# GpSimd's unit split moved to ScalarE and VectorE, and three adaLN units moved ahead of the odd layer

## The chip, the cores and the metric

One NeuronCore of a Trainium2 chip runs the whole kernel. The time is device microseconds of one execution. Engine names here: TensorE is PE, VectorE is DVE, ScalarE is ACT, GpSimd is POOL, and SP is the queue that issues the weight loads.

## What is computed

Two token streams, 128 context tokens and 256 latent tokens, pass through two trunk layers of width 1024. The kernel handles them together as 384 tokens, in float32. Every layer draws six modulation vectors per stream from an adaLN projection (`w_ada`, 1024 x 6144), then does a mixer and a squared-ReLU MLP:

```python
for li in range(DEPTH):                                        # DEPTH = 2
    sh1, sc1, g1, sh2, sc2, g2 = ada_mods(c, p['w_ada'][li], p['b_ada'][li])
    h = rms_norm(x, p['norm_w'][li, 0]) * (1 + sc1) + sh1
    if li % 2 == 0:
        y = even_layer(h)      # gated linear recurrence + windowed attention
    else:
        y = odd_layer(h)       # q, k, v = split_cols(h @ w_in_odd); differential attention, 8 heads
    x = x + g1 * y
    h = rms_norm(x, p['norm_w'][li, 1]) * (1 + sc2) + sh2
    x = x + g2 * sq_relu_mlp(h, p['w_mlp1'][li], p['w_mlp2'][li])
```

## The kernel before

**Units.** Every large weight is cut into units of 1024 x 256 (1 MB): 97 of them, numbered in order of use. Units 17 to 48 are the first MLP (four groups of eight), 49 to 60 the odd layer's input projection (q, k and v of four pairs of heads; "unit 0 of the odd layer" is 49), 61 to 64 its output projection, 65 to 96 the second MLP. Beside these there are 48 adaLN units of the same size, a0 to a47; a24 to a47 belong to the odd layer, and a36 to a47 (shift, scale and gate of its MLP) are used only behind its attention.

**A unit's way.** SP loads it into one of four places of `raw` (`load`, L468). A product is made at more than bfloat16 precision by splitting both factors into a high and a low part: the high part of the weights is a copy `wH <- raw` (ACT, `split_high`, L1035, and L1040 in the rows), the low part `wL = raw - wH` (DVE, `split_low`, L1486, L1493 in the rows), which raises the semaphore `w_split`. Then TensorE runs three passes over eight k tiles (`gemm_tiles`, L568; the rows' L594 for the "tok" form of 72 matmuls a unit, L589 for the other). `wH` and `wL` hold two units, so the split of unit u waits until the matmuls of unit u-2 are done. One unit of all is split by GpSimd: unit 50, `split` at L1956, called behind the last GpSimd work of the first MLP.

**An adaLN unit's way.** It needs no split: `ada_mm` (L604) runs 16 small matmuls from `raw` into a PSUM bank (OB for a0 to a35, TB for a36 to a47), ACT copies the row (`ada_copy`, L1046), `ada_turn` (L616) transposes it in two matmuls into TB, and DVE reduces it and adds the bias (`ada`, L1496: two small operations, L1505 and L1508). The copy on ACT frees the place in `raw`.

**The order of loads.** `STREAM` (L66 to L75) lists units and adaLN units in the order of loading; `POS` is the index in it. An item goes to place `pos % 4`. SP issues the loads one behind the other, each with a wait on the item four positions earlier: on `w_split` for a unit, on the copy of ACT for an adaLN unit. Around the change the list is 49, 50, a36, 51, a37, 52, a38, 53, and so on.

**Between the MLP and the odd layer.** DVE adds the last residual, ACT squares the last two tiles of x, TensorE sums the squares over the partitions with a matrix of ones (`last_norm_sums`, L637), ACT makes `rstd`. Then DVE's `modulate` (L1544) goes over eight tiles: `scaled_tile` (L1523, L1529 in the rows) multiplies, ACT's `shift` (L1090) adds and rounds to the high part of the operand, and `low_tile` (L1533, L1539 in the rows) makes its low part, which lets TensorE run that k tile of unit 49. The last residual waits on the last unit of the MLP, and so do ACT's and GpSimd's splits of unit 50.

**The odd layer's loop.** In each of its 12 units TensorE runs four k tiles, then turns and attention steps that are due, `ada_mm(36 + u)`, then the other four k tiles; the previous adaLN unit is turned behind the second k tile (L966 to L983). Attention of a pair of heads runs beside units 3 to 11. ACT and DVE have the same steps in the same order, each in its own loop (L1403, L1889).

Of the kernel before, what the change touches and what calls it, by code (L numbers as in the profile page):

```python
# [31 lines left out]
KT = D // P  # L32
# [36 lines left out]
    STREAM += [("a", _a) for _a in adas_of(_u)] + [("u", _u + 2)]  # L69
STREAM += [("a", _a) for _a in TAIL_ADAS]  # L70
STREAM += [("u", _u) for _u in range(15, U_ODD + 2)]
for _i in range(12):
    STREAM += [("a", 36 + _i), ("u", U_ODD + 2 + _i)]
STREAM += [("u", _u) for _u in range(U_ODD + 14, N_UNITS)]
POS = {item: n for n, item in enumerate(STREAM)}  # L75

POOL_UNITS = [U_ODD + 1]


def high_count(u):  # L80

    return u + 1 - sum(n <= u for n in POOL_UNITS)

# [73 lines left out]
def psum_uses():  # L159

    sc, tb, ob = [], ["vecs0", "vecs1"], []
    tb += [f"x{k}" for k in range(0, KT, 2)]
    sc += [f"x{k}" for k in range(1, KT, 2)] + ["norm0"]
    for a in ADA_FIRST:
        tb.append(f"ada{a}")
        ob.append(f"ada{a}")

    def even_jobs(jobs):
        for name in jobs:
            kind, i = job(name)  # L170
            if kind == "hg":
                sc.append(name)
            elif kind == "ada":
                ob.append(name)
            elif kind == "adt":
                tb.append(f"ada{i}")
            elif kind == "tq":
                sc.append(name)
            elif kind == "tk":
                tb.append("tk")  # L180
            elif kind == "swaA":
                if i >= 3:
                    ob.append(f"swaO{i - 3}")
                if i < N_SWA + 2:
                    tb.append(f"swaP{i - 2}.0")
            elif kind == "swaB":
                if i >= 2:
                    tb.append(f"swaP{i - 2}.1")
                if i < N_SWA:
                    sc.append(f"swa{i}")  # L190
            elif kind == "tile":
                sc.append(name)
                tb.append(f"turned{i}")
            elif kind == "state":
                ob.append(name)
            elif kind == "hgO":
                ob.append(name)
            elif kind == "hgN":
                tb.append(name)

    for jobs in EVEN_JOBS:
        even_jobs(jobs)
    even_jobs(EVEN_TAIL)
    sc.append("norm1")
    sc.append("norm2")

    def diff(s):
        if s >= 18 and norm_due(s):
            tb.append(f"dN{(s - 3) // 3}")
        if 2 <= s < N_DIFF + 2:  # L210
            tb.append(f"dP{s - 2}")
        if s < N_DIFF:
            sc.append(f"d{s}")
        if s >= 2 and (s - 2) % 3 == 2:
            ob.append(f"dO{(s - 2) // 3}")

    for u in range(13):
        for half in range(2):
            if half == 0 and u:
                tb.append(f"ada{35 + u}")  # L220
            if u < 12:
                tb.extend([f"dN{(s - 3) // 3}" for s in odd_slots(u, half) if norm_due(s)])
            if half == 0:
                tb.extend(odd_turns(u, 0))
                if u == 12:
                    tb.extend(odd_turns(u, 1))
            for s in odd_slots(u, half):
                diff(s)
            if u < 12:
                tb.extend(odd_turns(u, 1) if half else [f"adaM{36 + u}"])  # L230
    sc.append("norm3")
    tb.extend([f"y{k}" for k in range(KT)])
    return [{name: n for n, name in enumerate(uses)} for uses in (sc, tb, ob)]
# [31 lines left out]
def step_backbone_kernel(nc, t):  # L265
    ctx = ExitStack()
    with ctx:
# [157 lines left out]
            sem(n) for n in ("const_in", "x_in", "vec_in", "even_in", "odd_in", "out_dma", "kd_out"))  # L425
        raw_in = [sem(f"raw_in{i}") for i in range(RAW)]

        w_high, pool_high, w_split, gemm_done = (sem(n) for n in ("w_high", "pool_high", "w_split", "gemm_done"))

        g_free = [sem(f"g_free{i}") for i in range(2)]  # L430
        sc_full, sc_free = sem("sc_full"), sem("sc_free")
# [35 lines left out]
        def _(sp):  # L467
            def load(src, pos, wait=None):  # L468


                if wait is not None:
                    sp.wait_ge(*wait)
                elif pos >= RAW:
                    kind, n = STREAM[pos - RAW]
                    if kind == "u":
                        sp.wait_ge(w_split, n + 1)
                    elif n < 36:
                        sp.wait_ge(ob_free, OB_USE[f"ada{n}"] + 1)
                    else:
                        sp.wait_ge(tb_free, TB_USE[f"adaM{n}"] + 1)  # L480
                sp.dma_start(raw[:, pos % RAW, :, :], src).then_inc(raw_in[pos % RAW], 16)
# [73 lines left out]
        def _(pe):  # L555
# [48 lines left out]
            def ada_mm(a):  # L604

                pos = POS["a", a]
                buf, out, done, name = ("ob", OB, ob_full, "ada") if a < 36 else ("tb", TB, tb_full, "adaM")
                pe.wait_ge(raw_in[pos % RAW], 16 * (pos // RAW + 1))
                take(buf, f"{name}{a}")
                for k in range(KT):  # L610
                    j = k % 4
                    mm = pe.matmul(out[32 * j:32 * j + 32, 0:UC], cst[:, k, :], raw[:, pos % RAW, k, :],  # L612
                                   start=k < 4, stop=k >= 4, skip_group_check=True, tile_position=(0, 32 * j))
                mm.then_inc(done, 1)

            def ada_turn(a):  # L616

                if a < 36:
                    pe.wait_ge(ob_free, OB_USE[f"ada{a}"] + 1)
                take("tb", f"ada{a}")  # L620
                for i in range(2):
                    mm = turn(TB[:, P * i:P * i + P], adarow[:, P * i:P * i + P])
                mm.then_inc(tb_full, 1)
# [276 lines left out]
            with pe.Fori(0, 2) as g:  # L900
                mlp_group(U_MLP0 + 8, g, 2 * KT, 4, MLP0_ORDER)
            mlp_group(U_MLP0 + 24, 0, 2 * KT, 12, MLP0_ORDER)
            last_norm_sums(2)


            def diff_norm(s):
# [59 lines left out]
            for u in range(12):  # L966
                for half in range(2):
                    middle = {}
                    if u and half == 0:
                        middle[1] = lambda: ada_turn(35 + u)  # L970
                    if odd_slots(u, half):
                        middle[2] = lambda: diff_norm(odd_slots(u, half)[0])
                    gemm_half(U_ODD + u, half, "tok", (opH, opL), op_ready(3 * KT) if u == 0 else None,
# [2 lines left out]
                        turns(u, 0)  # L976
                    for s in odd_slots(u, half):
                        diff(s)
                    if half == 0:
                        ada_mm(36 + u)  # L980
                    else:
                        turns(u, 1)
            ada_turn(47)  # L983
            turns(12, 0)
            turns(12, 1)

# [29 lines left out]
        def _(act):  # L1016
# [27 lines left out]
                    split_high(u, POS["u", u])  # L1044

            def ada_copy(a):  # L1046
                if a < 36:
                    full("ob", f"ada{a}")
                    act.activation(adarow[:, :], OB[:, 0:UC], ACT.Copy).then_inc(ob_free, 1)
                else:  # L1050
# [270 lines left out]
            def mlp_group(base, g, pos, n_hid, last, turned_out=None, finish=None):  # L1321


                for i in range(8):
# [17 lines left out]
                        split_high(u + 2, pos + i + 2, g)  # L1342
                    if turned_out is not None and i > 4:
                        turned_out(2 * (i - 5) + 1)
                    if finish is not None and i >= 4:
                        finish(u, 2 * (i - 4))

# [4 lines left out]
            with act.Fori(0, 2) as g:  # L1352
                mlp_group(U_MLP0 + 8, g, b0 + 8, 4, False)
            mlp_group(U_MLP0 + 24, 0, b0 + 24, 12, False,
                      finish=lambda u, tile0: squares(2, u, tile0))
            norm_rstd(2)
            shift(2)


            act.wait_ge(lamr_set, 1)  # L1360
# [42 lines left out]
            for u in range(12):  # L1403
# [2 lines left out]
                turned(u, 0)  # L1406
                for s in odd_slots(u, 0):
                    diff(s)
                ada_copy(36 + u)
                for s in odd_slots(u, 1):  # L1410
                    diff_norm(s)
                g = unit_out(U_ODD + u, "tok")
# [60 lines left out]
        def _(dve):  # L1473
# [12 lines left out]
            def split_low(u, g=0, pos=None):  # L1486

                pos = POS["u", u] if pos is None else pos
                dve.wait_ge(w_high, high_count(u) + 8 * g)
                if u - 1 in POOL_UNITS:  # L1490

                    dve.wait_ge(w_split, u)
                dve.tensor_tensor(wL[:, u % 2, :, :], raw[:, pos % RAW, :, :], wH[:, u % 2, :, :].bitcast(F32),  # L1493
                                  ALU.subtract).then_inc(w_split, 1)

# [45 lines left out]
                                                   opH[:, q, a:b].bitcast(F32), ALU.add, ALU.subtract)  # L1541
                ins.then_inc(op_set, 1)

            def modulate(n, n_op):  # L1544

                dve.wait_ge(rstd_set, n + 1)
                for k in range(KT + 1):
                    if k < KT:
                        scaled_tile(n, n_op, k)
                    if k:  # L1550
                        low_tile(n, n_op, k - 1)

# [300 lines left out]
                mlp_group(0, U_MLP0 + 8, g, b0 + 8, 4, False)  # L1853
            mlp_group(0, U_MLP0 + 24, 0, b0 + 24, 12, False, 2)
            scales(2, 32)
            modulate(2, 3 * KT)


            dve.wait_ge(odd_in, 16 * 3)
# [29 lines left out]
            for u in range(12):  # L1889
# [6 lines left out]
                    dve.wait_ge(g_free[(U_ODD + u) % 2], (U_ODD + u) // 2 + 1)  # L1896
                for s in odd_slots(u, 1):
                    diff(s)
                ada(36 + u)
                split_low(U_ODD + u + 2)  # L1900
                if part < 2:
                    qk_scale(draw[:, part, :], 3 + 2 * j + part + 1, 12)
# [27 lines left out]
        def _(pool):  # L1930
# [21 lines left out]

            settle(pool.tensor_scalar(wrow[:, 2, :], wrow[:, 2, :], HD ** -0.5, None, ALU.mult))
            settle(tables(ropeE, 0))

            def split(u):  # L1956


                pos = POS["u", u]
                pool.wait_ge(raw_in[pos % RAW], 16 * (pos // RAW + 1))  # L1960
                if u >= 2:
                    pool.wait_ge(gemm_done, u - 1)
                pool.tensor_scalar(wH[:, u % 2, :, :], raw[:, pos % RAW, :, :], 1.0, None, ALU.mult).then_inc(pool_high, 1)
                pool.wait_ge(pool_high, POOL_UNITS.index(u) + 1)

                pool.wait_ge(w_split, u)
                pool.tensor_tensor(wL[:, u % 2, :, :], raw[:, pos % RAW, :, :], wH[:, u % 2, :, :].bitcast(F32),
                                   ALU.subtract).then_inc(w_split, 1)

            def keys(u):  # L1970

# [81 lines left out]
            with pool.Fori(0, 4) as g:  # L2053
                relu_squares(U_MLP0, g, 0)

            split(U_ODD + 1)

            pool.wait_ge(rope_tab, 1)
            for j in range(4):
                for part in range(2):  # L2060
# [80 lines left out]
```

## Time and profile before

| | before |
|---|---|
| median of 3 runs | 1167.46 us (1167.18 to 1168.17) |
| profiled execution | 1167.8 us |
| its span | 1165.7 us |
| PE busy | 1054.6 us (90%), 7330 matmuls |
| DVE busy | 571.7 us (49%) |
| ACT busy | 486.8 us (42%) |
| POOL busy | 144.5 us (12%) |
| mean granted TensorE clock | 0.966 of full |
| loads | 160.38 MB moved, mean 138 GB/s |

Times in rows are microseconds from the start of the span. "Idle before <-releaser" says how long an engine had nothing to do ahead of a row, and whose work let it go on. "Landing" is the time from the issue of a load until its data is there. PEclk is the granted clock: 1.00 is 2.4 GHz, 0.50 is 1.2 GHz.

### The profile page before, as it was taken

The numbers are of one execution on the slowest core, as the hardware profiler recorded it, in microseconds if no ns is written. First come the engines' busy times: TensorE is split into PE (matmuls) and PEld (weight loads), VectorE is DVE, ScalarE is ACT, GpSimd is POOL, SyncE is SP. The second block draws the span as 40 slices with busy tenths as digits, with TensorE's granted clock in tenths as the row PEclk, the third lists the DMA queues.
The fourth block names the chain that finished last, engine by engine and source line by source line (L and its number), as shares of the span: only waits on it lengthen the run. The fifth ranks groups of instructions, "written<-read, shape, count | busy, mean of one in ns | idle before, by whom it ended". The sixth has DMA issues, their size and how long they took to land.

```text
span 1165.7 us, 17989 instructions
## 1 busy us (share of the span) xinstructions
PE 1054.6 (90%) x7330; PEld 963.1 (83%) x7330; DVE 571.7 (49%) x906; ACT 486.8 (42%) x858; POOL 144.5 (12%) x170
## 2 busy tenths in 40 slices
PE   5798677788889999999996998999789999999998
PEld 2686455667789999999996987777579999999997
DVE  2543535655346544445456535555645544445452
ACT  4345344434435425243343535555535414334241
POOL 0051101000010102010013123113000101011010
PEclk9999898899999999999999999999889999999999
DMA  8865333366462443434332444443213343434321
GB/s 284 279 200 207 109 109 109 112 238 208 149 222 81 137 145 109 144 109 136 116 129 90 144 155 144 145 150 120 83 39 107 123 138 109 138 111 140 110 72 55
DMA packets 157099, 160.38 MB, mean 138 GB/s; under 512 B 3627, under 2 KB 155717, under 8 KB 157029
## 3 DMA queue, kind: packets, MB, share of 16 engines
q1 hardware_dynamic: 155028, 156.50, 40.9%
q0 software_dynamic: 528, 1.70, 0.4%
q10 hardware_dynamic: 1472, 1.18, 0.3%
q8 instruction: 52, 0.85, 0.3%
q14 instruction: 19, 0.15, 0.0%
HBM read 156.09 MB, written 3.28 MB: 137 GB/s over the span
## 4 chain that ended last, share of the span: by engine, by line
PE 76%; ACT 12%; DVE 7%; issue 4%; DMA 0%; SPq 0%; ACTq 0%; DVEq 0%
PE G L589 54%; PE G L594 10%; ACT wH L1040 3%; PE OB L612 3%; PE TB L563 3%; DVE wL L1493 1%; PE OB L946 1%; PE OB L792 1%; PE TB L612 1%; DVE small L1731 1%; PE SC L632 1%; DVE nbuf L1529 1%; ACT hq L1187 1%; PE SC L675 1%; PE SC L681 1%
## 5 line engine op out<-in xcount | busy, mean ns | idle before, releaser
L589 PE MATMUL G<-opH,wH 128*128 128x386 f32 (+1 forms) x768 | 273.2, 356 | 5.5 <-DVE wL L1493 3.1
L589 PE MATMUL G<-opH,wL 128*128 128x386 f32 (+1 forms) x768 | 264.8, 345 | 0.0
L589 PE MATMUL G<-opL,wH 128*128 128x386 f32 (+1 forms) x768 | 264.7, 345 | 0.0
L1040 ACT ACTIVATE wH<-raw 128x2048 fp32r<-128x2048 f32 x96 | 183.3, 1910 | 186.8 <-PE G L589 182.7
L1493 DVE TENSOR_TENSOR wL<-raw,wH 128x2048 fp32r<-128x2048 f32 x96 | 221.1, 2303 | 80.9 <-ACT wH L1040 80.9
L589 PE MATMUL G<-hidH,wH 128*128 128x384 f32 x512 | 172.5, 337 | 0.0
L589 PE MATMUL G<-hidH,wL 128*128 128x384 f32 x512 | 172.1, 336 | 0.0
L589 PE MATMUL G<-hidL,wH 128*128 128x384 f32 x512 | 172.1, 336 | 0.0
L589 PEld LDWEIGHTS G<-opH,wH 128*128 128x128 f32 x768 | 148.6, 194 | 16.9 <-issue 8.5
L589 PEld LDWEIGHTS G<-opL,wH 128*128 128x128 f32 x768 | 148.4, 193 | 0.9
L589 PEld LDWEIGHTS G<-opH,wL 128*128 128x128 f32 x768 | 148.4, 193 | 0.0
L594 PE MATMUL G<-wH,opH 128*128 128x256 f32 x408 | 124.7, 306 | 15.1 <-DVE opL L1539 13.9
L594 PE MATMUL G<-wH,opL 128*128 128x256 f32 x408 | 117.2, 287 | 0.0
L594 PE MATMUL G<-wL,opH 128*128 128x256 f32 x408 | 116.9, 287 | 0.0
L1584 DVE SCALAR_TENSOR_TENSOR xT<-G,mods,xT 128x128 f32<-128x128 f32 (+1 forms) x160 | 55.7, 411 | 124.2 <-PE G L589 124.2
L2050 POOL TENSOR_TENSOR relu<-relu 128x768 f32<-128x768 f32 x32 | 47.0, 1469 | 535.7 <-ACT relu L1336 535.7
L1336 ACT ACTIVATE relu<-relu,small 128x128 f32<-128x128 f32 (+1 forms) x128 | 48.0, 447 | 150.9 <-DVE relu L1833 150.9
L594 PEld LDWEIGHTS G<-wH,opH 128*128 128x128 f32 x408 | 79.7, 195 | 27.6 <-issue 20.4
L589 PEld LDWEIGHTS G<-hidL,wH 128*128 128x128 f32 x512 | 96.3, 188 | 0.0
L589 PEld LDWEIGHTS G<-hidH,wH 128*128 128x128 f32 x512 | 96.3, 188 | 0.0
L589 PEld LDWEIGHTS G<-hidH,wL 128*128 128x128 f32 x512 | 96.2, 188 | 0.0
L594 PEld LDWEIGHTS G<-wH,opL 128*128 128x128 f32 x408 | 79.7, 195 | 0.7
(244 smaller groups left out, 1161.5 us busy)
## 6 DMA issues: line engine op xcount, KB each, us to landing
raw<-in_w_mlp SPq DMA_DIRECT2D x64, 1024.0 KB, 5.2
raw<-in_w_ada SPq DMA_DIRECT2D x48, 1024.0 KB, 6.3
raw<-in_w_in_even SPq DMA_DIRECT2D x13, 1024.0 KB, 6.5
raw<-in_w_in_odd SPq DMA_DIRECT2D x12, 1024.0 KB, 5.0
raw<-in_w_out_even SPq DMA_DIRECT2D x4, 1024.0 KB, 5.3
raw<-in_w_out_odd SPq DMA_DIRECT2D x4, 1024.0 KB, 5.2
xin<-in_x_sample SPq DMA_DIRECT2D x1, 1024.0 KB, 6.4
out_y_sample<-yout SPq DMA_DIRECT2D x1, 768.0 KB, 4.0
```

The costliest lines, as they stand in the source:

```text
L563: return pe.transpose(out, src, ident[0:n, 0:n])
L589: mm = pe.matmul(G[:, s, 512 * m:512 * m + cols], w[:, s, k, P * m:P * m + P], a[:, k, 0:cols], start=first and q == 0, stop=last and q == 2)
L594: mm = pe.matmul(G[:, s, UC * tt:UC * tt + UC], a[:, k, P * tt:P * tt + P], w[:, s, k, :], start=first and q == 0 and tt != 1, stop=last a ...
L612: mm = pe.matmul(out[32 * j:32 * j + 32, 0:UC], cst[:, k, :], raw[:, pos % RAW, k, :], start=k < 4, stop=k >= 4, skip_group_check=True, ti ...
L632: mm = pe.matmul(SC[:, 0:NTOK], ones[:, :], rstd[:, :] if k == 5 else nbuf[:, k % 2, :], start=k == 5, stop=k == KT - 1)
L675: mm = pe.matmul(SC[:, P * m:P * m + P], hq[:, n, :], joined(n, 2 ** lev), start=True, stop=True, skip_group_check=True)
L681: mm = pe.matmul(SC[c:c + 32, 32 * m:32 * m + 32], k, q, start=True, stop=True, skip_group_check=True, tile_position=(0, c))
L1040: act.activation(wH[:, u % 2, :, :], raw[:, pos % RAW, :, :], ACT.Copy).then_inc(w_high, 1)
L1336: ins = act.activation(part, part, ACT.Relu, bias=shifts[:, u % 2, m, c:c + 1])
L1493: dve.tensor_tensor(wL[:, u % 2, :, :], raw[:, pos % RAW, :, :], wH[:, u % 2, :, :].bitcast(F32), ALU.subtract).then_inc(w_split, 1)
L1584: ins = dve.scalar_tensor_tensor(xT[:, k, a:b], G[:, u % 2, 512 * m + a:512 * m + b], mods[:, layer, KT * gate + k, c:c + 1], xT[:, k, a:b ...
L2050: pool.tensor_tensor(relu2[:, u % 2, :], relu[:, u % 2, :], relu[:, u % 2, :], ALU.mult).then_inc(relu2_set, 1)
```

## The change

Unit 50 is split by ACT (high part, in the last unit of the first MLP, ahead of the last two squares) and by DVE (low part, behind the whole modulation). GpSimd splits nothing. Three adaLN units, a36 to a38, are computed between the first MLP and the odd layer, with bank OB instead of TB: TensorE puts a36 between the sums of squares and a37, a38 behind them; ACT copies them around `norm_rstd` and the first shifts; DVE takes a36 ahead of the modulation and a37 and a38 within it. The odd layer's loop does a39 to a47 in its units 0 to 8, none in 9 to 11. `STREAM` follows: 49, 50, a36, a37, a38, 51, a39, 52, a40, 53 and so on.

```diff
@@ STREAM
 STREAM += [("u", _u) for _u in range(15, U_ODD + 2)]
+STREAM += [("a", 36), ("a", 37), ("a", 38)]
 for _i in range(12):
-    STREAM += [("a", 36 + _i), ("u", U_ODD + 2 + _i)]
+    STREAM += [("u", U_ODD + 2 + _i)] + ([("a", 39 + _i)] if _i < 9 else [])
...
@@ SP, load
                     if kind == "u":
                         sp.wait_ge(w_split, n + 1)
-                    elif n < 36:
+                    elif n < 39:
                         sp.wait_ge(ob_free, OB_USE[f"ada{n}"] + 1)
...
@@ TensorE, behind the first MLP
-            last_norm_sums(2)
+            norm_sum(2, 5)
+            ada_mm(36)
+            norm_sum(2, 6)
+            norm_sum(2, 7)
+            ada_turn(36)
+            ada_mm(37)
+            ada_turn(37)
+            ada_mm(38)
...
@@ TensorE, the odd layer's loop
-                    if u and half == 0:
-                        middle[1] = lambda: ada_turn(35 + u)
+                    if u <= 9 and half == 0:
+                        middle[1] = lambda: ada_turn(38 + u)
...
-                    if half == 0:
-                        ada_mm(36 + u)
-                    else:
+                    if half:
                         turns(u, 1)
-            ada_turn(47)
+                    elif u < 9:
+                        ada_mm(39 + u)
...
@@ ACT, mlp_group
+                    if finish is not None and i == 7:
+                        split(U_ODD + 1)
                     if finish is not None and i >= 4:
                         finish(u, 2 * (i - 4))
...
+            ada_copy(36)
             norm_rstd(2)
-            shift(2)
+            ada_copy(37)
+            shift(2, range(2))
+            ada_copy(38)
+            shift(2, range(2, KT))
...
@@ DVE
-            def modulate(n, n_op):
+            def modulate(n, n_op, adas):
                 dve.wait_ge(rstd_set, n + 1)
                 for k in range(KT + 1):
                     if k < KT:
                         scaled_tile(n, n_op, k)
+                    if k in adas:
+                        ada(adas[k])
                     if k:
                         low_tile(n, n_op, k - 1)
...
             scales(2, 32)
-            modulate(2, 3 * KT)
+            ada(36)
+            modulate(2, 3 * KT, {1: 37, 4: 38})
+            split_low(U_ODD + 1)
...
@@ GpSimd
-            split(U_ODD + 1)
```

## Rows read from the trace of the kernel before

**Rows 1.** page, part 4: the chain that ended last, its share of the span by engine
```profile
PE 76%; ACT 12%; DVE 7%; issue 4%; DMA 0%; SPq 0%; ACTq 0%; DVEq 0%
```

**Rows 2.** chain of waits, 628 to 700: start us, us, engine, output and line, count
```profile
634.37 0.81 DVE nbuf L1529 x3
...
635.29 4.72 DVE nbuf L1529
...
640.82 7.12 PE G L594 x36
647.94 1.00 PE TB L612 x16
...
659.09 1.07 PE TB L612 x16
...
670.56 1.07 PE TB L612 x16
```

**Rows 3.** timeline, 618 to 665, ACT, then GpSimd: start, us, engine, operation, count [idle before <-releaser]
```profile
621.27 1.92 ACT L1040 ACTIVATE wH<-raw 128x2048 fp32r<-128x2048 f32 x1 [5.58 <-PE G L589]
623.09 0.92 ACT L1057 ACTIVATE nbuf<-xT 128x384 f32<-128x384 f32 x2
630.96 0.94 ACT L1057 ACTIVATE nbuf<-xT 128x384 f32<-128x384 f32 x2 [6.95 <-DVE xT L1584]
...
653.45 0.81 ACT L1418 ACTIVATE dsq<-G 128x768 f32<-128x768 f32 x1 [1.92 <-PE G L594]
...
629.66 5.36 POOL L1963 TENSOR_SCALAR wH<-raw 128x2048 fp32r<-128x2048 f32 x1 [29.32 <-PE G L589]
635.11 4.63 POOL L1967 TENSOR_TENSOR wL<-raw,wH 128x2048 fp32r<-128x2048 f32 x1
```

**Rows 4.** timeline of VectorE, 640 to 690
```profile
639.94 0.74 DVE L1539 SCALAR_TENSOR_TENSOR opL<-nbuf,mods,opH 128x128 fp32r<-128x128 f32 x2
640.71 0.75 DVE L1529 SCALAR_TENSOR_TENSOR nbuf<-xT,scale,rstd 128x128 f32<-128x128 f32 x2
...
649.55 0.75 DVE L1539 SCALAR_TENSOR_TENSOR opL<-nbuf,mods,opH 128x128 fp32r<-128x128 f32 x2 [0.22 <-ACT opH L1096]
...
655.93 0.17 DVE L1505 TENSOR_REDUCE small<-TB 128x4 f32<-128x16 f32 x1
...
656.79 2.29 DVE L1493 TENSOR_TENSOR wL<-raw,wH 128x2048 fp32r<-128x2048 f32 x1 [0.49 <-ACT wH L1040]
```

**Rows 5.** timeline of the SP queue, 590 to 720: the issues of weight loads
```profile
625.53 0.37 SPq L481 DMA_DIRECT2D raw<-in_w_ada  x1
639.76 0.37 SPq L481 DMA_DIRECT2D raw<-in_w_in_odd  x1
...
659.11 0.37 SPq L481 DMA_DIRECT2D raw<-in_w_in_odd  x1
```

**Rows 6.** loads issued at 72.4 and 72.8, then 84.7 and 85.1: us to landing, min/median/max
```profile
L481 SPq DMA_DIRECT2D raw<-in_w_ada x2: 367/474/582, 72.4 to 72.8; - x2
...
DMA to landing us min/median/max: 5.4/6.6/7.7
...
DMA to landing us min/median/max: 5.1/6.2/7.3
```

**Rows 7.** windows: us, PE, PEld, DVE, ACT, POOL busy, PEclk, DMA share, GB/s
```profile
56.00:57.00 1.00, 0.84 (x4) 0.84 (x5) 0.80 (x3) 0.02 (x1) 0.00 (x0) 0.58 1.01 323
59.00:60.00 1.00, 1.00 (x8) 1.00 (x8) 0.00 (x0) 0.00 (x0) 0.66 (x2) 0.72 1.09 388
636.00:637.00 1.00, 0.00 (x0) 0.00 (x0) 1.00 (x1) 0.00 (x0) 1.00 (x1) 0.71 0.00 0
646.00:647.00 1.00, 1.00 (x8) 1.00 (x7) 0.96 (x4) 0.62 (x2) 0.00 (x0) 0.67 0.00 0
```

**Rows 8.** chain of waits, 762 to 862, units 9 to 11 of the odd layer
```profile
777.50 1.00 PE TB L612 x16
...
798.20 0.28 ACT adarow L1052
```

More of the change, by code:

```diff
@@ L71 @@
 STREAM += [("u", _u) for _u in range(15, U_ODD + 2)]
+STREAM += [("a", 36), ("a", 37), ("a", 38)]
 for _i in range(12):
-    STREAM += [("a", 36 + _i), ("u", U_ODD + 2 + _i)]
+    STREAM += [("u", U_ODD + 2 + _i)] + ([("a", 39 + _i)] if _i < 9 else [])
 STREAM += [("u", _u) for _u in range(U_ODD + 14, N_UNITS)]
 POS = {item: n for n, item in enumerate(STREAM)}
-POOL_UNITS = [U_ODD + 1]
 def high_count(u):
-    return u + 1 - sum(n <= u for n in POOL_UNITS)
+    return u + 1
 N_HG = 2 * (LEVELS + 1)
@@ L205, in psum_uses @@
     sc.append("norm2")
+    for a in (36, 37, 38):
+        ob.append(f"ada{a}")
+        tb.append(f"ada{a}")
     def diff(s):
@@ L218, in psum_uses @@
         for half in range(2):
-            if half == 0 and u:
-                tb.append(f"ada{35 + u}")
+            if half == 0 and 1 <= u <= 9:
+                tb.append(f"ada{38 + u}")
             if u < 12:
@@ L229, in psum_uses @@
             if u < 12:
-                tb.extend(odd_turns(u, 1) if half else [f"adaM{36 + u}"])
+                tb.extend(odd_turns(u, 1) if half else [f"adaM{39 + u}"] if u < 9 else [])
     sc.append("norm3")
@@ L426, in step_backbone_kernel @@
         raw_in = [sem(f"raw_in{i}") for i in range(RAW)]
-        w_high, pool_high, w_split, gemm_done = (sem(n) for n in ("w_high", "pool_high", "w_split", "gemm_done"))
+        w_high, w_split, gemm_done = (sem(n) for n in ("w_high", "w_split", "gemm_done"))
         g_free = [sem(f"g_free{i}") for i in range(2)]
@@ L606, in ada_mm @@
                 pos = POS["a", a]
-                buf, out, done, name = ("ob", OB, ob_full, "ada") if a < 36 else ("tb", TB, tb_full, "adaM")
+                buf, out, done, name = ("ob", OB, ob_full, "ada") if a < 39 else ("tb", TB, tb_full, "adaM")
                 pe.wait_ge(raw_in[pos % RAW], 16 * (pos // RAW + 1))
@@ L616, in ada_turn @@
             def ada_turn(a):
-                if a < 36:
+                if a < 39:
                     pe.wait_ge(ob_free, OB_USE[f"ada{a}"] + 1)
@@ L1046, in ada_copy @@
             def ada_copy(a):
-                if a < 36:
+                if a < 39:
                     full("ob", f"ada{a}")
@@ L1408, in _ @@
                     diff(s)
-                ada_copy(36 + u)
+                if u < 9:
+                    ada_copy(39 + u)
                 for s in odd_slots(u, 1):
@@ L1489, in split_low @@
                 dve.wait_ge(w_high, high_count(u) + 8 * g)
-                if u - 1 in POOL_UNITS:
-                    dve.wait_ge(w_split, u)
                 dve.tensor_tensor(wL[:, u % 2, :, :], raw[:, pos % RAW, :, :], wH[:, u % 2, :, :].bitcast(F32),
@@ L1898, in _ @@
                     diff(s)
-                ada(36 + u)
+                if u < 9:
+                    ada(39 + u)
                 split_low(U_ODD + u + 2)
@@ L1954, in _ @@
             settle(tables(ropeE, 0))
[L1956 to L1968, printed above, removed]
             def keys(u):
```

## The prediction

> **What bounds the kernel now.** I read the page first: the chain that ended last is TensorE for 76% of the span, and ACT, VectorE (DVE) and issue for nearly all the rest [rows 1]. TensorE alone is therefore the measure: a change pays where it shortens a stretch in which TensorE is idle or does extra work, and costs where TensorE waits longer. The chain in order of time then shows the stretch that the change touches [rows 2]. The last MLP matmul ends near 629.5, DVE starts the modulation at 634.37, one DVE operation of that group takes 4.72 us, and the first matmul of the odd layer starts at 640.82. It runs four k tiles until 647.94, then the adaLN unit 36 (16 matmuls), then the rest. The timelines of ACT and GpSimd say what lies beside it [rows 3]: GpSimd splits unit 50 from 629.66 to 639.74. The SP queue's timeline says which load goes out when [rows 5].
>
> **Part 1, GpSimd's split goes: a gain before the odd layer.** The slow DVE operation (L1529, 128x256) takes 4.72 us while GpSimd's two-input subtract runs (635.11 to 639.74); a pair of the same line (128x128 and 128x256) takes 0.75 us once GpSimd is quiet [rows 2 to 4]. It ends when GpSimd ends. Two pairs would need 2 x 0.75, overlapped by a little, so 1.4 us instead of the 5.6 from 634.37 to 640.0: 4.1 us less.
> The Trainium skill, page "SBUF — State Buffer", section "SBUF: two separate sides", says the same: the port pair of DVE and GpSimd is an exclusive lock, and a DVE operation with two SBUF inputs blocks for a whole GpSimd instruction. The trace agrees (4.72 us). A reading that stops there forecasts 4.1 us of gain and nothing else.
>
> **Part 2, ACT takes the high split of unit 50.** It stands before the last two squares. It waits for the end of unit 48, as GpSimd did. In the group before, the squares follow a split 1.82 us after its start (621.27, 623.09) [rows 3]. A split from 629.6 puts the squares at 631.42 instead of 630.96: 0.46 us later, all of it on the path square, sum, rstd, modulation. DVE then starts at 634.37 + 0.46 = 634.83.
>
> **Part 3, three adaLN units in the gap.** On TensorE unit 36 fits between the sums (one takes 1.00 [rows 2]; TensorE idles there), and 37 and 38 run while DVE modulates. The copies on ACT fall into its waits. DVE's share is two small operations, 655.93 to about 656.3 [rows 4], 0.35 us each unit. Unit 36 lies in the wait for rstd: free. Unit 37 stands before the first low tile and 38 after the fifth scaled tile: 0.35 each on the DVE path. The first low tile starts at 634.83 + 1.4 + 0.35 = 636.6 (before 639.94 [rows 4]), so TensorE could start the odd layer 3.4 us earlier.
>
> **Part 4, DVE takes the low split, behind the modulation.** Before, the modulation ran from the first low tile at 639.94 to the end of the last, 649.55 + 0.75 = 650.30 [rows 4], 10.36 us. Now: 636.6 + 10.36 + 0.35 (unit 38) = 647.3, and the split, 2.29 us [rows 4], ends at T = 649.6. Before, GpSimd had it done at 639.74. If the adaLN unit 38 reaches DVE late, because TensorE turns it only after its second k tile, T is up to 1 us later.
>
> **Part 5, what is queued behind that split: the term that decides.** SP issues the weight loads strictly in the order of STREAM, and each waits until the item four places earlier is used up. Before, the order was 49, 50, a36, 51, a37, 52: the load of a36 needed nothing of unit 50. The load behind unit 50's split was unit 52, issued at 639.76, 0.02 after GpSimd's end [rows 3, 5], with time to spare. Now the order is 49, 50, a36, a37, a38, 51, a39, 52, a40. Unit 51 stands four behind unit 50, so its load waits for T. a39 needs only a36, long done, but it stands behind 51 in SP's queue. And TensorE runs a39 in the middle of the first unit of the odd layer (unit 49), where a36 ran. TensorE finishes its first four k tiles by about 644 at the latest and then stands. a38's load, last issued before, goes out at 625.53 as a37's did [rows 5] and is in time.
> The landing: of two loads issued 0.4 us apart the second landed 7.7 us after its issue, the first 5.4 (issued at 72.4 and 72.8); in another such pair 5.1 and 7.3 [rows 6]. I take 7.5, with 7.3 and 7.7 as ends. a39: 649.6 + 0.03 + 0.4 + 7.5 = 657.5. The same place in the kernel before is 647.94 [rows 2]: **+9.6 us**. The gain of parts 1 to 3 is gone with it: it only lengthens the stand.
> Two more loads (52, a40) are issued at once behind a39. The Trainium skill, page "DMA: Bandwidth & Descriptors", section "Queues, rings and completion order", says that each DMA engine takes descriptors in ring order, so they should not delay a39; the pair of 72.4 had a third load behind it as well and still landed in order. Without ring order a39 would land up to about 5.5 us later (a rival below).
>
> **Part 6, TensorE's clock.** The granted clock is half (1.2 of 2.4 GHz) after the gap of the kernel before: it fell within 636 to 637, while TensorE waited for the modulation, and rose within 646 to 647, though TensorE was at work from 640.82: 5.9 us of work at half rate [rows 2, 7]. That cost lay in the first four k tiles. Now the stand of 13 us or more falls behind them, so the clock falls again and a39 and the second half of unit 49 (36 matmuls, from 648.94 to ACT's start on it at 653.45 [rows 2, 3]) pay it: 5.9 / 2 = 2.9 us. The nearest short case is 56 to 60 us, about 3.2 us at half: 1.6 [rows 7]. I take **2.9**, since the idle before it is like the long one; ends 1.6 and 3.0.
>
> **Part 7, what goes out of the last three units.** Units 9 to 11 of the odd layer lose their adaLN matmuls, and 10 and 11 their turns. On the chain there: 1.00 at 777.50, the same once more in unit 11, 0.28 of ACT's copy at 798.20 [rows 8] and one turn of about 0.2. The third set of matmuls (unit 10) is hidden behind DVE and ACT, and so is the last turn. **-2.5 us**; ends -1.0 (TensorE waits for ACT and DVE instead) and -3.0. Units 1 to 8 keep one adaLN unit each. The tightest is now that of unit 2: its load follows that of unit 53, which went out at 659.11 (behind unit 51's split), and TensorE wants it at 670.56 [rows 2, 5], 11.4 us later where 0.4 + 7.5 are needed: no wait, nothing.
>
> **Sum.** +9.6 + 2.9 - 2.5 = +10.0 us on the profiled execution (1167.8, span 1165.7): 1177.8. The median before is 1167.46, 0.3 lower; so 1177.5.
>
> **Rivals.**
> (a) The load is in time, and the kernel is faster. It decides at about 643.5: a39 must have landed when TensorE's fourth k tile is done, so its load must be out by 636, before DVE has even begun the low tiles. Then TensorE starts 3.4 us earlier, but in unit 50 it waits for ACT, which stands at unit 51's load (landing 649.6 + 5, split until 656.5) before it copies the turned keys; before, that wait ended at 659.09 [rows 2] and now near 658.6. So -0.5, and with part 7 -3.0: 1164.5. For it speaks only that I could misread the order; the measured 0.02 from split to load speaks against.
> (b) The loads share the engines evenly. Each further 1 MB moved the landing by about 2.7 us (72.4 + 5.4 to 72.8 + 7.7) [rows 6]; a39 would land with the fourth, 5.5 us later: 1183.0. The landings in order speak against.
> (c) The removed work of part 7 gives 1 us alone, or the clock stays low for the short spell: 1179.0 and 1176.2, both within my case's own range.
> (d) The stand is shorter by some overlap that I don't see and the two gains nearly cancel it, within 0.2% of before: a39 would have to start by 651, when its load is hardly out.
>
> **How the numbers follow.** My case 0.80, (a) 0.06, (b) 0.08, (d) 0.03, and 0.03 for a larger loss still. My case's own range: low 9.3 + 1.6 - 3.0 = +7.9, high 10.8 + 3.0 - 1.0 = +12.8, so 1175.4 to 1180.3. For 8 in 10 with room for (b) I give 1174.0 to 1183.0. 0.2% is 2.3 us, about what a measurement of this kernel can tell from no change. Faster 0.06, same 0.03, slower 0.91.
>
> **What would show it.** Right: SP's load of unit 51 within 0.1 us behind DVE's split near 649.6, and not at 617; TensorE idle from about 643 until near 657.5 in front of the adaLN matmuls; half clock behind it; DVE's L1529 at 0.75 a pair; first matmul of the layer near 637.3. Wrong: the adaLN matmuls in unit 49 before 650 (part 5), a39 landing after 660 (b), full clock behind the stand (part 6), units 9 to 11 no shorter (part 7).

## The result, and the profile after

The changed kernel took 1175.74 us (median of 8 runs, 1171.59 to 1179.99), the kernel before 1167.14 (median of 8, 1163.04 to 1170.68). The ratio is 1.0086, 95% interval 1.0065 to 1.0108: slower by 10.0 us (0.0086 x 1167; the ratio compares runs of the same chip, and the two medians differ by 8.6). The profiled execution took 1179.53 with a span of 1177.6. Line numbers have moved: L1504 is the low split (before L1493), L1540 the scaled tile (L1529), L1550 the low tile (L1539), L613 the adaLN matmuls (L612), L595 the "tok" matmuls (L594), L1047 the high split (L1040).

The page of the kernel after, span and busy time. Nothing of it says where 12 us of span went: TensorE does 1.8 us more and GpSimd 10 us less than before.

```profile
span 1177.6 us, 17991 instructions
...
PE 1056.4 (90%) x7330; PEld 962.7 (82%) x7330; DVE 567.2 (48%) x907; ACT 487.8 (41%) x859; POOL 134.3 (11%) x168
```

To compare two executions, one must first take out what lies ahead of the change. Both kernels have the same program up to the last residual of the first MLP, but for the order in which SP takes its last loads. That residual starts at 629.53 before and at 632.06 after (VectorE's timelines: before's row is in the next fence, after's is the first row of the one behind it), 2.53 us apart. The change hardly made this: the variants below whose program is the changed kernel's up to there start it between 625.93 and 628.93. I call this start R, and count from it.

```profile
629.53 1.39 DVE L1584 SCALAR_TENSOR_TENSOR xT<-G,mods,xT 128x128 f32<-128x128 f32 x4 [2.89 <-PE G L589]
630.84 2.48 DVE L1516 SCALAR_TENSOR_TENSOR scale<-mods,vecs 128x16 f32<-128x16 f32 x1
```

VectorE's timeline of the kernel after, start and duration in front. It answers to [rows 2, 4].

```profile
632.06 1.39 DVE L1597 SCALAR_TENSOR_TENSOR xT<-G,mods,xT 128x128 f32<-128x128 f32 x4 [2.89 <-PE G L590]
633.37 0.16 DVE L1527 SCALAR_TENSOR_TENSOR scale<-mods,vecs 128x16 f32<-128x16 f32 x1
...
637.26 1.41 DVE L1540 SCALAR_TENSOR_TENSOR nbuf<-xT,scale,rstd 128x128 f32<-128x128 f32 x4 [0.52 <-ACT rstd L1076]
...
638.88 0.75 DVE L1550 SCALAR_TENSOR_TENSOR opL<-nbuf,mods,opH 128x128 fp32r<-128x128 f32 x2
...
648.77 0.75 DVE L1550 SCALAR_TENSOR_TENSOR opL<-nbuf,mods,opH 128x128 fp32r<-128x128 f32 x2 [0.21 <-ACT opH L1103]
649.44 2.28 DVE L1504 TENSOR_TENSOR wL<-raw,wH 128x2048 fp32r<-128x2048 f32 x1
```

The four scaled operations take 1.41 us instead of 5.65, as GpSimd is quiet. GpSimd's copy had slowed VectorE too: the small operation for the scales (L1516, L1527 after) takes 0.16 us instead of 2.48, and 2.48 again in e3 below, where GpSimd splits. That cost nothing before, since it ended at 633.32 and the scaled operations wait for `rstd` until 634.37. But the split of unit 50 comes last and ends at 651.72, which is R + 19.7; before, GpSimd's ended at R + 10.2 [rows 3].

The SP queue's timeline, which answers to [rows 5]: the load of unit 51, a39, unit 52, a40.

```profile
651.75 0.37 SPq L482 DMA_DIRECT2D raw<-in_w_in_odd  x1
652.16 0.58 SPq L482 DMA_DIRECT2D raw<-in_w_ada  x1
652.79 1.54 SPq L482 DMA_DIRECT2D raw<-in_w_in_odd  x1
654.37 2.63 SPq L482 DMA_DIRECT2D raw<-in_w_ada  x1
```

Unit 51's load goes out 0.03 us behind the end of the split, and a39's 0.4 behind that. The two answers of the trace on landing, first for the loads of 651.75 and 652.16 (min, median, max), then for those of 652.79 and 654.37:

```profile
DMA to landing us min/median/max: 5.2/6.3/7.5
...
DMA to landing us min/median/max: 9.5/10.1/10.7
```

They landed at 657.0, 659.7, 662.3 and 665.1: one behind the other, 2.7 us apart. TensorE's timeline: the first k tile of unit 49, the last matmul of its fourth, and a39.

```profile
639.77 0.35 PE L595 MATMUL G<-wH,opH 128*128 128x256 f32 x1 [0.56 <-DVE opL L1550]
...
645.34 0.28 PE L595 MATMUL G<-wL,opH 128*128 128x256 f32 x1
...
659.69 1.94 PE L613 MATMUL TB<-raw,cst 128*32 128x256 f32 x16 [14.07 <-DMA raw<-in_w_ada]
```

The view of who waited for whom, TensorE from 640 to 670 (us in total, times, longest):

```profile
PE TB L613 <- DMA raw<-in_w_ada: 14.1, 1, 14.1
```

This is the cost of the change in one line: TensorE starts the odd layer at R + 7.7 (before R + 11.3), and then stands 14.07 us, until the data of a39 are there. The windows (columns as in [rows 7]) show the clock: full (1.00) in the first k tiles, falling in the stand, half when TensorE resumes, full again from 665.3 (0.84 as the mean of its window).

```profile
639.00:640.00 1.00, 0.44 (x6) 0.26 (x3) 0.96 (x4) 0.80 (x3) 0.00 (x0) 1.00 0.00 0
648.00:649.00 1.00, 0.00 (x0) 0.00 (x0) 0.79 (x3) 0.74 (x2) 0.00 (x0) 0.63 0.00 0
664.00:665.00 1.00, 1.00 (x7) 1.00 (x6) 0.00 (x0) 0.00 (x0) 0.00 (x0) 0.50 0.38 132
665.00:666.00 1.00, 1.00 (x9) 1.00 (x9) 0.00 (x0) 0.00 (x0) 0.00 (x0) 0.84 0.00 0
```

### The profile page after: what moved, and what is told of

The parts are those of the page before. It is cut to its first block and busy times, and to the rows that moved or that the text cites. A ratio compares the mean times of both kernels' runs of the same rounds, so it can differ in the third digit from the quotient of the medians.

```text
span 1177.6 us, 17991 instructions
## 1 busy us (share of the span) xinstructions
PE 1056.4 (90%) x7330; PEld 962.7 (82%) x7330; DVE 567.2 (48%) x907; ACT 487.8 (41%) x859; POOL 134.3 (11%) x168
## 5 line engine op out<-in xcount | busy, mean ns | idle before, releaser
L1047 ACT ACTIVATE wH<-raw 128x2048 fp32r<-128x2048 f32 x97 | 185.1, 1909 | 193.2 <-PE G L590 189.1
L1504 DVE TENSOR_TENSOR wL<-raw,wH 128x2048 fp32r<-128x2048 f32 x97 | 223.3, 2302 | 84.0 <-ACT wH L1047 84.0
L595 PE MATMUL G<-wH,opH 128*128 128x256 f32 x408 | 124.4, 305 | 8.3 <-DVE opL L1550 7.1
L595 PE MATMUL G<-wH,opL 128*128 128x256 f32 x408 | 117.1, 287 | 0.0
L595 PE MATMUL G<-wL,opH 128*128 128x256 f32 x408 | 116.8, 286 | 0.0
L595 PEld LDWEIGHTS G<-wH,opH 128*128 128x128 f32 x408 | 79.4, 195 | 20.6 <-issue 12.4
L595 PEld LDWEIGHTS G<-wH,opL 128*128 128x128 f32 x408 | 79.6, 195 | 0.7
```

The costliest lines, as they stand in the source:

```text
L595: mm = pe.matmul(G[:, s, UC * tt:UC * tt + UC], a[:, k, P * tt:P * tt + P], w[:, s, k, :], start=first and q == 0 and tt != 1, stop=last a ...
L1047: act.activation(wH[:, u % 2, :, :], raw[:, pos % RAW, :, :], ACT.Copy).then_inc(w_high, 1)
```

## The experiments

Every count below is from R of its own execution. "End of unit 49" is the start of ACT's first operation on it, [rows 3] before and the last row here of after; the first two rows are ACT's split of unit 50 and the squares behind it.

```profile
632.12 1.91 ACT L1047 ACTIVATE wH<-raw 128x2048 fp32r<-128x2048 f32 x1 [5.58 <-PE G L590]
633.94 0.92 ACT L1064 ACTIVATE nbuf<-xT 128x384 f32<-128x384 f32 x2
...
667.78 0.81 ACT L1432 ACTIVATE dsq<-G 128x768 f32<-128x768 f32 x1 [5.70 <-PE G L595]
```

| kernel | R | first matmul of unit 49 | end of unit 49 | ratio of times to before, 95% |
|---|---|---|---|---|
| before | 629.53 | 11.3 | 23.9 | 1 |
| after | 632.06 | 7.7 | 35.7 | 1.0086 (1.0065 to 1.0108) |
| e1_split_first | 625.93 | 7.7 | 19.1 | 0.9914 (0.9892 to 0.9935) |
| e2_port_only | 631.30 | 8.9 | 20.7 | 0.9948 (0.9933 to 0.9963) |
| e3_pool_keeps_split | 628.51 | 11.5 | 24.8 | 0.9981 (0.9961 to 1.0001) |
| e4_a39_before_51 | 627.03 | 7.7 | 33.3 | 1.0041 (1.0019 to 1.0063) |
| e5_busy_stand | 628.93 | 7.7 | 34.7 | 1.0092 (1.0059 to 1.0124) |
| e6_gap_busy | 620.61 | 7.7 | 18.8 | 0.9954 (0.9932 to 0.9977) |
| e7_busy_to_landing | 627.54 | 7.7 | 33.2 | 1.0080 (1.0051 to 1.0109) |

**One edit that removes the stand.** DVE is free between its last residual and rstd, so its split fits there.

```diff
             scales(2, 32)
+            split_low(U_ODD + 1)
             ada(36)
             modulate(2, 3 * KT, {1: 37, 4: 38})
-            split_low(U_ODD + 1)
```

> The changed kernel with one edit: DVE makes the low part of unit 50 before the modulation, not behind it. Theory (the load of a39 waits for that split): DVE is free between its last residual and rstd, the split ends about 634 in the time frame of the kernel before (17 us earlier than in the changed kernel), a39 lands near 642, before TensorE's fourth k tile is done near 643, and the stand of 14 us is gone. TensorE then follows DVE's modulation, ends unit 49 about 5.3 us earlier than the kernel before, and with 2.6 us from units 9 to 11 the whole is about 8 us faster than before: 1159, ratio 0.993. Rival (the moved adaLN units and the DVE split themselves cost the time, wherever they stand): it stays within 2 us of the changed kernel, ratio 1.007 to 1.01.

It took 1155.57 us (before on the same chip 1166.14): ratio 0.9914. VectorE's timeline, with the residual and the split, then TensorE's row of a39's matmuls, then ACT's start on unit 49:

```profile
625.93 1.39 DVE L1597 SCALAR_TENSOR_TENSOR xT<-G,mods,xT 128x128 f32<-128x128 f32 x4 [2.89 <-PE G L590]
...
628.00 2.29 DVE L1504 TENSOR_TENSOR wL<-raw,wH 128x2048 fp32r<-128x2048 f32 x1 [0.60 <-ACT wH L1047]
```

```profile
639.44 1.07 PE L613 MATMUL TB<-raw,cst 128*32 128x256 f32 x16
```

```profile
645.00 0.81 ACT L1432 ACTIVATE dsq<-G 128x768 f32<-128x768 f32 x1 [0.38 <-PE G L595]
```

The split now ends at 630.3 (R + 4.4), the loads go out behind it, and a39's matmuls at 639.44 have no wait in front of them. The end of unit 49 is 16.6 us earlier than in the changed kernel, and the first matmul of unit 49 starts no later (R + 7.7 in both). So the moved adaLN units and the DVE split are not what cost the time; the rival has fallen. The gain over the kernel before is 10.0 us (7.6 to 12.6) where 8 was expected; from R to the end of the span the two profiled executions differ by 7.5. Beside e2, which lacks the adaLN units in the gap, e1's median is 4.5 us lower. From R to the first matmul of the output projection their traces differ by 3.1 of it (196.6 and 199.7): 1.6 at the end of unit 49, and 1.5 behind it. Units 9 to 11 are 2.9 us shorter, but e2 has no spell of half clock near 700 and e1 has one. This kernel, with one line moved, beats both.

**The port alone.** The kernel before, with only the split moved.

```diff
-POOL_UNITS = [U_ODD + 1]
+POOL_UNITS = []
...
+                    if finish is not None and i == 7:
+                        split(U_ODD + 1)
                     if finish is not None and i >= 4:
                         finish(u, 2 * (i - 4))
...
             scales(2, 32)
+            split_low(U_ODD + 1)
             modulate(2, 3 * KT)
...
-            split(U_ODD + 1)        # GpSimd
```

> The kernel before with the split of unit 50 alone moved: ACT's part in the last unit of the first MLP, DVE's part before the modulation, GpSimd splits nothing, adaLN units and load order as before. Port theory: L1529 falls from 4.72 to about 0.4 us, the odd layer starts about 3.6 us earlier (4.1 less the 0.46 of ACT's split), and the time is 3.5 to 5 us below before: 1162 to 1164, ratio 0.996. Rival (GpSimd's split hid behind other work): within 1 us of before.

0.9948, 6.1 us faster (4.3 to 7.8), where 3.5 to 5 was expected. VectorE's timeline: the residual, and the four scaled operations, 1.41 us. Then the window that starts at 640:

```profile
631.30 1.39 DVE L1586 SCALAR_TENSOR_TENSOR xT<-G,mods,xT 128x128 f32<-128x128 f32 x4 [2.89 <-PE G L589]
...
637.73 1.41 DVE L1531 SCALAR_TENSOR_TENSOR nbuf<-xT,scale,rstd 128x128 f32<-128x128 f32 x4 [2.06 <-ACT rstd L1069]
```

```profile
640.00:641.00 1.00, 0.76 (x3) 0.80 (x4) 0.96 (x4) 0.10 (x2) 0.00 (x0) 0.50 0.04 12
```

The port theory holds: 5.65 us of the four operations have become 1.41. The modulation starts later here than after an undisturbed sum (R + 6.4, not 5.2), because in this execution the clock had fallen already in the sums of squares: it is half (0.50) from R + 2.7 on, and the last two sums take 2.79 us instead of 1.56. It is still half in the first k tiles of unit 49. So the first matmul of unit 49 comes 2.4 us earlier than before, not 3.6; the end of unit 49 comes 3.2 earlier, and the stretch from R to the end of the span is 4.3 us shorter. Why the whole time gained 6.1 is open.

**The same new order with GpSimd's split.** The function `split` and its semaphore come back with it; they are left out here.

```diff
+POOL_UNITS = [U_ODD + 1]
...
-                    if finish is not None and i == 7:
-                        split(U_ODD + 1)
...
             ada(36)
             modulate(2, 3 * KT, {1: 37, 4: 38})
-            split_low(U_ODD + 1)
...
+            split(U_ODD + 1)        # GpSimd
```

> The changed kernel with the split of unit 50 given back to GpSimd; the three adaLN units and the new load order stay. Theory (the end of that split sets the stand): the split ends at 639.7 in the frame of the kernel before, a39 lands near 647.7, TensorE arrives there at 647 to 648, so the stand is 0 to 1.5 us, not 14. With 2.6 us from units 9 to 11: 1 to 3 us below before, ratio 0.998. Rival (the new load order or the adaLN units in the gap cost the time themselves): 7 us or more above before.

0.9981 (0.9961 to 1.0001), as expected, though the interval just takes in no change. VectorE, GpSimd, the SP queue (unit 51, a39) and TensorE (a39's matmuls):

```profile
628.51 1.39 DVE L1600 SCALAR_TENSOR_TENSOR xT<-G,mods,xT 128x128 f32<-128x128 f32 x4 [2.89 <-PE G L593]
...
633.27 5.66 DVE L1543 SCALAR_TENSOR_TENSOR nbuf<-xT,scale,rstd 128x128 f32<-128x128 f32 x4 [0.52 <-ACT rstd L1079]
```

```profile
634.08 4.56 POOL L1985 TENSOR_TENSOR wL<-raw,wH 128x2048 fp32r<-128x2048 f32 x1
```

```profile
638.67 0.37 SPq L485 DMA_DIRECT2D raw<-in_w_in_odd  x1
639.09 0.58 SPq L485 DMA_DIRECT2D raw<-in_w_ada  x1
```

```profile
647.70 1.07 PE L616 MATMUL TB<-raw,cst 128*32 128x256 f32 x16 [0.61 <-DMA raw<-in_w_ada]
```

The price of the port is back (5.66 us), the split ends at 638.64 (R + 10.1), the loads go out behind it instead of at R + 19.7, and the stand is 0.61 us. Unit 49 ends 0.9 us later than before. The granted clock fell in this longer gap, though the adaLN units ran in it: half from R + 9.5 to R + 16.3. So the order of loads and the adaLN units cost no more than this 0.9 us while the split ends early, and units 9 to 11 are 1.4 us shorter than before, though a half-clock spell (798 to 802) lies in them.

**Which of the waiting loads comes first.**

```diff
 for _i in range(12):
     STREAM += [("u", U_ODD + 2 + _i)] + ([("a", 39 + _i)] if _i < 9 else [])
+    if _i == 0:
+        STREAM[-2:] = STREAM[:-3:-1]
```

> The changed kernel with the first pair of the new load order swapped: a39 ahead of unit 51. Both still wait for the split of unit 50. Theory (ring order: a39 lands first of the four loads issued together): landing 5.1 us after its issue, not 7.5, issue 0.4 us earlier, so the stand is 2.8 us shorter and the time 2.8 us below the changed kernel: ratio to before 1.006. Rival (the loads share the engines evenly): no difference to the changed kernel.

TensorE's row of a39's matmuls, and the trace's answer on its load:

```profile
652.07 1.93 PE L615 MATMUL TB<-raw,cst 128*32 128x256 f32 x16 [11.48 <-DMA raw<-in_w_ada]
```

```profile
L484 SPq DMA_DIRECT2D raw<-in_w_ada x1: 368/368/368, 646.7 to 646.7; - x1
...
DMA to landing us min/median/max: 5.3/5.3/5.3
```

The load lands 5.3 us after its issue instead of 7.5, and the stand is 11.48 us, 2.6 less; unit 49 ends 2.4 us earlier. The time is 1.0041 of before, 4.5 in 1000 (5 us) under the changed kernel, of which the trace shows 2.4 us; the intervals of the two ratios lie just apart, so the size of the gain in the whole time is uncertain. Loads that share the engines evenly would have landed a39 hardly earlier. The Trainium skill, page "DMA: Bandwidth & Descriptors", section "Queues, rings and completion order", has each DMA engine take its descriptors in ring order; this run agrees (a39 lands 5.3 us after its issue as the first of the four loads, 7.5 us as the second).

**The clock in the stand.** 18 extra matmuls before a39 (e5), then 22 (e7, the same edit with 22 for 18):

```diff
                     elif u < 9:
+                        if u == 0:
+                            pe.wait_ge(sc_free, SC_USE["norm2"] + 1)
+                            for _ in range(18):
+                                pe.matmul(SC[:, 0:NTOK], ones[:, :], xT[:, 0, :], start=True, stop=True)
                         ada_mm(39 + u)
```

> The changed kernel with 18 extra matmuls of ones and a tile of x (results unused) in TensorE's stand in front of a39's adaLN matmuls, some 12 us of work at 0.66 us each. Theory (clock term): the granted clock stays full through the stand, the adaLN matmuls take 1.07 instead of 1.94 us and the second half of unit 49 4.3 instead of 6.2 us, so the time is 2.7 us below the changed kernel: ratio to before 1.006. Rival (the clock does not follow TensorE's idleness here): half clock behind the landing as before, no difference to the changed kernel. Rival 2 (the extra work runs past the landing): up to 1 us of the gain is lost.

> As e5_busy_stand with 22 extra matmuls: 18 lasted 10.9 us and left TensorE idle for 2.3 us before the landing, and the clock was at half behind it. 22 last 13.3 us and reach the landing. Theory (clock term of the stand): full clock through the second half of unit 49, whose end comes 33.0 us behind the start of the last residual (35.7 in the changed kernel, 34.7 with 18), so 2.7 us less there. The whole time may hide this, since other half-clock spells move it by as much. Rival: half clock behind the landing again, 34.7 or more.

With 18, TensorE ran dry 2.34 us before the landing, and the clock fell within 0.2 us of its resuming (a mean of 0.78 in that window). TensorE's row of a39's matmuls, and the windows of the resuming and behind it:

```profile
656.44 1.88 PE L613 MATMUL TB<-raw,cst 128*32 128x256 f32 x16 [2.34 <-DMA raw<-in_w_ada]
```

```profile
656.00:657.00 1.00, 0.56 (x8) 0.36 (x12) 0.00 (x0) 0.00 (x0) 0.00 (x0) 0.78 1.08 386
657.00:658.00 1.00, 1.00 (x15) 0.22 (x5) 0.00 (x0) 0.00 (x0) 0.00 (x0) 0.50 1.09 387
```

With 22:

```profile
655.21 1.07 PE L613 MATMUL TB<-raw,cst 128*32 128x256 f32 x16
```

```profile
656.00:657.00 1.00, 1.00 (x14) 0.79 (x7) 0.00 (x0) 0.39 (x1) 0.00 (x0) 1.00 1.09 387
```

The adaLN matmuls take 1.88 us at half and 1.07 at full clock, and unit 49 ends at R + 34.7 and R + 33.2, where 35.7 is the changed kernel's. The extra work of e7 reaches the landing and doesn't run past it: a39's matmuls start at R + 27.7, against R + 27.6 without it. The clock's term is thus 2.5 us, 1.4 of it lost again where the extra work stops too early. In the whole time it can't be seen: 1.0092 and 1.0080 against 1.0086. Of e5 the expectation of 1.006 failed. Its profiled execution was at half clock from 830 to 848, behind the odd layer's loop, where the changed kernel's was from 832 to 840; that such spells hide the gain in the other executions too is not shown.

**The clock in the gap.** The kernel of e2, with 2 extra matmuls between the sums and 5 behind them:

```diff
-            last_norm_sums(2)
+            norm_sum(2, 5)
+            busy(2)
+            norm_sum(2, 6)
+            norm_sum(2, 7)
+            busy(5)
```

> The kernel with only the split moved (e2_port_only) and 7 extra matmuls (results unused) in TensorE's idle time between the first MLP and the odd layer, 2 between the sums and 5 behind them, where the changed kernel has its adaLN units. Theory (the adaLN units in the gap keep the clock up): full clock through unit 49, its end 18.4 us behind the start of the last residual instead of 20.7, the time 2.3 us below that kernel, ratio to before 0.993. Rival (no effect of the clock, unit 49 follows DVE's modulation anyway): 20.7 and 0.995 again.

VectorE's residual (R) and ACT's start on unit 49:

```profile
620.61 1.39 DVE L1595 SCALAR_TENSOR_TENSOR xT<-G,mods,xT 128x128 f32<-128x128 f32 x4 [2.89 <-PE G L589]
```

```profile
639.38 0.81 ACT L1429 ACTIVATE dsq<-G 128x768 f32<-128x768 f32 x1 [0.37 <-PE G L594]
```

Unit 49 ends at R + 18.8, 1.9 us earlier than in the profiled execution of e2, and the clock is full throughout. But the ratio, 0.9954, is that of e2 (0.9948), and the expected 0.993 did not come. The profiled execution of e2 was the slowest of its 11 (1164.99, median 1160.03), so it may be that the clock falls in this gap in some executions only. The effect is shown for two executions, not for the mean.

## Why the prediction was right

It gave 1177.5, range 1174.0 to 1183.0, slower; the median is 1175.74. By its steps, each from R:

- **The port (part 1).** 4.1 us predicted (its own 5.6 and 1.4 give 4.2); the four operations went from 5.65 to 1.41, 4.2. Right.
- **ACT's split (part 2).** 0.46 predicted; the modulation starts at R + 5.20 instead of R + 4.84: 0.36. Right.
- **The adaLN units in the gap (part 3).** First matmul 3.4 us earlier predicted, 3.6 measured. What the step did not say: the clock was full in the first four k tiles, at half before [rows 7]. It was so in every profiled execution that had these units in the gap and no GpSimd split (after, e1, e4, e5, e7). With the split (e3), where the gap is 11.5 us, it fell again, and without the units (e2, a gap of 8.9) too. In none of these traces did it hold without the work in the gap.
- **The end of the split (part 4).** 649.6 predicted in the time frame of before; 651.72 - 2.53 = 649.2. Right.
- **The load behind it (part 5).** 7.5 us to landing predicted, 7.5 measured; a39's matmuls start at R + 27.6 (659.69 - 632.06) instead of a36's at R + 18.3 (before's row is below): +9.3, where +9.6 was predicted, 0.4 of it since the split ended that much earlier than it had said. The experiments set the end of the split to R + 4.4, R + 10.1 and R + 19.7, and the stand was none, 0.61 and 14.07 us. This is the cause.

```profile
647.87 1.07 PE L612 MATMUL TB<-raw,cst 128*32 128x256 f32 x16
```

- **The clock (part 6).** 2.9 predicted. The end of unit 49 moved by 35.7 - 23.9 = 11.8, so 2.5 on top of the 9.3; e7, with the stand kept busy, measures 2.5 too. Right, 0.4 too large. (Its low end, 1.6, came from a spell of "about 3.2 us"; [rows 7] give 3.4, so 1.7.)
- **The last three units (part 7).** -2.5 predicted. ACT's starts on units 8 to 11 of the odd layer, before and then after:

```profile
768.12 0.81 ACT L1421 ACTIVATE dv<-G 128x768 f32<-128x768 f32 x1
...
783.00 0.81 ACT L1418 ACTIVATE dsq<-G 128x768 f32<-128x768 f32 x1 [3.73 <-PE G L594]
...
798.36 0.82 ACT L1418 ACTIVATE dsq<-G 128x768 f32<-128x768 f32 x1
...
815.01 0.81 ACT L1421 ACTIVATE dv<-G 128x768 f32<-128x768 f32 x1
```

```profile
782.68 0.81 ACT L1435 ACTIVATE dv<-G 128x768 f32<-128x768 f32 x1
...
796.36 0.81 ACT L1432 ACTIVATE dsq<-G 128x768 f32<-128x768 f32 x1 [2.81 <-PE G L595]
...
811.45 0.81 ACT L1432 ACTIVATE dsq<-G 128x768 f32<-128x768 f32 x1
...
826.70 0.81 ACT L1435 ACTIVATE dv<-G 128x768 f32<-128x768 f32 x1
```

The three steps are 14.9, 15.4 and 16.7 us before, and 13.7, 15.1 and 15.3 after: -2.9. Over the whole stretch from the end of unit 49 to the first matmul of the output projection it is 180.24 against 177.66: -2.6, as some 0.3 us came in elsewhere.

Sum from R to the end: 1177.6 - 632.06 = 545.5 against 1165.7 - 629.53 = 536.2, +9.4. The ratio gives +10.0 (7.6 to 12.6), the medians +8.6; predicted +10.0. The mechanism and its steps came out; that the total agrees with the ratio to 0.1 us is luck, since the steps measured in the trace add up to 9.3 + 2.5 - 2.6 = 9.2. Rival (a) fell: the load was late, as the order of the queue said. Its side was real only when the split stood elsewhere, as e1 shows, and there the gain was larger than its 3 us: unit 51's load went out at R + 4.4, and the 4.8 us by which unit 49 ends earlier than before are still there at the end of unit 50 (R + 30.3 against 35.1). Rival (b), loads that share evenly, fell with the landings 2.7 us apart and with e4. Nothing came of (c) or (d).

## What to carry to other kernels

When work moves from one engine to another, ask first which queue waits for its end, and what stands behind that wait: here a split that no matmul needed before the end of unit 49 held back a load that TensorE needed in the middle of it. A load order with four buffers ties each load to the release four places earlier; move two items (here a37 and a38) ahead of another, and its wait falls on another item. A gain of a port or an engine upstream of a stand only makes the stand longer; take the stand away, and the same gains count (e1).

## What the runs showed of the hardware that was not expected

- The same program up to R, but for the order of the last loads, reached it at 620.61 us in one execution (e6) and at 632.06 in another (after), with the others between. In the one of 620.61 the granted clock was half for about 27 us ahead of R, in the one of 632.06 for about 44, but others with 48 reached it at 626 (e1) and 630 (before). So the clock accounts for a part, and the rest is open. Counting from R takes this part out, but not the half-clock spells behind R, 23 to 42 us in sum: from R to the end the profiled executions of e1 to e4 differ from before by -7.5, -4.3, +1.1 and +7.1 us, where their ratios give -10.0, -6.1, -2.2 and +4.8. So two single executions of this kernel don't settle 3 us over the whole span; a stretch such as that from R to the end of unit 49, whose clock one can read, does.
- The clock stayed full through the gap of 7.7 us (from R to the first matmul of unit 49) when seven short matmuls (e6) or three adaLN units lay in it, fell in the gap of 8.9 us without either (e2), and fell in the gap of 11.5 us of e3 in spite of the adaLN units.
- Four loads of 1 MB, issued within 2.6 us, land one behind the other, 2.7 us apart. A place further ahead in the queue gave a39 2.2 us from its own issue, and 2.6 us of stand (e4).
- VectorE waited for GpSimd beside both of its operations, but not all the time: beside the copy (L1963) a small operation took 2.48 us instead of 0.16, while the three scaled pieces at 634.37, beside the copy's end, took 0.81 us together [rows 2]; the piece beside the subtract took 4.72. The profiler's spans of GpSimd are rough, so where exactly the copy lets go stays open.
